# Last delta head: the first half of the output weights folded by GpSimd, and four output products in front of the keys

## The reference

```
qkv = silu(causal_conv4(proj[q, k, v]));  z = proj[z]
q, k = l2norm(q) * 128**-0.5, l2norm(k)
o = chunk_gated_delta_rule(q, k, v, g, beta)            # 8 heads of 128
o = o * rsqrt(mean(o * o) + eps) * onorm_g * silu(z)
out = o.reshape(S, 8 * 128) @ gdn_out_w                 # 1024 x 1024
x = x + gate * out                                      # gate: one row of 1024
```

## Time and profile before

| what | value |
|---|---|
| median of three runs | 2266.24 us (2265.8 to 2268.85) |
| profiled execution | 2268.18 us, span in the trace 2266.1 us |
| TensorE busy | 2176.8 us, 96% |
| VectorE busy | 1311.4 us, 58% |
| ScalarE busy | 593.0 us, 26% |
| GpSimd busy | 172.3 us, 8% |
| head 7 of the delta block | about 1078 to 1220 us of the span |

### The profile page before, as it was taken

How to read it: one execution, slowest core, us unless ns; L and a number is a source line. 1 busy time by engine, 2 the same in 40 slices (tenths; PEclk the granted TensorE clock), 3 DMA queues, 4 the chain that set the end, 5 groups by cost and what they waited for, 6 DMA issues and landing times. The chain is left out here.

```text
span 2266.1 us, 20611 instructions
## 1 busy us (share of the span) xinstructions
PE 2176.8 (96%) x7098; PEld 1120.0 (49%) x7098; DVE 1311.4 (58%) x1833; ACT 593.0 (26%) x960; POOL 172.3 (8%) x135
## 2 busy tenths in 40 slices
PE   6999999989999999999999999999999999999998
PEld 5444444346656656556454455544444444444443
DVE  4687733264664664764823676377469998341333
ACT  4355522233333443443213320121100000230012
POOL 0000000122212212211100000000000000000000
PEclk8999999999999999999999999999999999999999
DMA  9333420121111111111410344321111111015001
GB/s 324 114 110 116 130 103 0 74 65 37 34 26 43 29 33 39 35 32 38 130 32 19 121 64 59 78 76 33 42 33 47 33 33 47 28 37 197 26 19 56
DMA packets 200911, 146.86 MB, mean 65 GB/s; under 512 B 49997, under 2 KB 171906, under 8 KB 200834
## 3 DMA queue, kind: packets, MB, share of 16 engines
q1 hardware_dynamic: 186417, 144.14, 21.6%
q10 hardware_dynamic: 14048, 0.85, 0.4%
q0 software_dynamic: 384, 1.05, 0.2%
HBM read 126.45 MB, written 18.38 MB: 64 GB/s over the span
## 5 line engine op out<-in xcount | busy, mean ns | idle before, releaser
L2095 PE MATMUL bank<-hT,ring 128*128 128x512 f32 x1472 | 637.4, 594 | 2.5 <-DMA ring<-in_w_in 2.5
L2095 PEld LDWEIGHTS bank<-hT,ring 128*128 128x128 f32 x1472 | 279.6, 190 | 352.9 <-issue 349.2
L2756 DVE SCALAR_TENSOR_TENSOR yT<-s_arena,yT 128x1024 f32<-128x1024 f32 x240 | 308.3, 1285 | 8.4
L1235 PE MATMUL bank<-hT,ring 128*128 128x512 f32 x336 | 162.2, 595 | 1.8 <-ACT silu_z L1465 1.8
L2095 PE MATMUL bank<-yT,ring 128*128 128x512 f32 x256 | 110.0, 592 | 0.0
L1810 DVE SCALAR_TENSOR_TENSOR memory<-memory,col_exp_last,bank 128x128 f32<-128x128 f32 x64 | 22.2, 347 | 137.8 <-PE bank L1410 137.8
L2095 PE MATMUL bank<-ssm_y,ring 128*128 128x512 f32 x192 | 83.9, 592 | 0.6 <-DVE s_arena L2770 0.6
L1235 PE MATMUL bank<-resid,yT 128*128 128x512 f32 x168 | 82.5, 593 | 0.0
L2095 PEld LDWEIGHTS bank<-yT,ring 128*128 128x128 f32 x256 | 48.6, 190 | 61.2 <-issue 61.2
L1235 PEld LDWEIGHTS bank<-hT,ring 128*128 128x128 f32 x336 | 56.8, 193 | 36.1 <-issue 36.1
L2399 ACT ACTIVATE s_arena<-bank 128x1024 f32<-128x1024 f32 x8 | 8.2, 1023 | 242.5 <-PE bank L2095 242.5
(11 more groups left out here) (533 smaller groups left out, 3354.4 us busy)
## 6 DMA issues: line engine op xcount, KB each, us to landing
ring<-in_w_in SPq DMA_DIRECT2D x48, 512.0 KB, 3.7
ada<-in_ada_w SPq DMA_DIRECT2D x8, 2048.0 KB, 8.0
ring<-in_gdn_in_w SPq DMA_DIRECT2D x32, 512.0 KB, 4.1
resid<-in_x SPq DMA_DIRECT2D x8, 1024.0 KB, 8.8
ring<-in_lru_in_w SPq DMA_DIRECT2D x16, 512.0 KB, 3.7
lru_arena<-in_ada_w SPq DMA_DIRECT2D x6, 1024.0 KB, 13.1
x_scratch<-resid SPq DMA_DIRECT2D x2, 2048.0 KB, 10.6
decayT<-g_scratch SPq DMA_DIRECT2D x8, 512.0 KB, 4.3
```

The source lines that it names most:

```text
L1235: last = nc.tensor.matmul(bank[:, to, :], w[:, k, :], v[:, k, :], start=(first and k == 0), stop=(k == KB - 1), skip_group_check=not only)
L2095: last = nc.tensor.matmul(bank[:, 2 * PAIR[name] + h, :], w[:, k, :], src[:, k, h * HALF:(h + 1) * HALF], start=(k == 0), stop=(k == kt - 1))
L2756: dve_b.mark(dve.scalar_tensor_tensor(out=yT[:, n, :], in0=padded[:, p, j:j + S], scalar=taps[:, p, j:j + 1], in1=yT[:, n, :], op0=ALU.mul ...
```

## The change

VectorE no longer folds the first half. GpSimd does it, in four operations: tiles 0 and 1 and tiles 2 and 3 after its work for head 6, then the causal addition of head 7, then tiles 4 and 5, then tile 6, then the masks of head 7. Each of the three DMAs of `out_w0` gets a semaphore of its own (`out0_loaded`), each fold raises `folded` by one, and TensorE waits for `folded` at the products k = 0, 2, 4 and 6 of group 0. The first fill of a head, in front of the wait for the keys, takes four products in head 7 instead of none; the other fills keep their counts. GpSimd's `body` is split, so that the masks can be called apart.

```diff
             out_loaded = [sem(f"gdn_out_loaded{n}") for n in range(5)]
+            out0_loaded = [sem(f"gdn_out0_loaded{n}") for n in range(3)]
+            folded = sem("gdn_out0_folded")
...
-                        sp.dma_start(out_w0[:, 2 * b:2 * b + 2, :], out_w[:, 2 * b:2 * b + 2, 0:HALF]).then_inc(out_loaded[0], 16)
+                        sp.dma_start(out_w0[:, 2 * b:2 * b + 2, :], out_w[:, 2 * b:2 * b + 2, 0:HALF]).then_inc(out0_loaded[b], 16)
...
-                    body(HEADS - 1, False, False)
+                    gate = gate_b[:, 1, 0:HALF]
+                    for b in range(2):
+                        g.wait_ge(out0_loaded[b], 16)
+                        g.tensor_tensor(out_w0[:, 2 * b:2 * b + 2, :], out_w0[:, 2 * b:2 * b + 2, :],
+                                        gate.unsqueeze(1).broadcast_to([P, 2, HALF]), ALU.mult).then_inc(folded, 1)
+                    hd_dve.wait(g, "rel", HEADS - 1)
+                    hd_pool.mark(g.tensor_tensor(decayT[:, :, :], decayT[:, :, :], along(causal[:, :]), ALU.add), "rel")
+                    g.wait_ge(out0_loaded[2], 16)
+                    g.tensor_tensor(out_w0[:, 4:6, :], out_w0[:, 4:6, :], gate.unsqueeze(1).broadcast_to([P, 2, HALF]), ALU.mult).then_inc(folded, 1)
+                    g.wait_ge(out_loaded[1], 16)
+                    g.tensor_tensor(out_w6, out_w6, gate, ALU.mult).then_inc(folded, 1)
+                    masks(HEADS - 1)
...
-                            if n == 0:
-                                dve_f.wait(pe, "fold0")
                             if n == TT:
                                 dve_f.wait(pe, "fold1")
                             for k in range(KT - 1):
-                                if (n, k) == (0, 6):
-                                    dve_f.wait(pe, "fold6")
+                                if n == 0 and k % 2 == 0:
+                                    pe.wait_ge(folded, k // 2 + 1)
...
-                        fill(4, 0)
+                        fill(4, 4)
...
-                            fold("fold0", out_w0, gates[0].unsqueeze(1).broadcast_to([P, 6, HALF]), 0, 3)
-                            fold("fold6", out_w6, gates[0], 1, 1)
```

More of the change, by code:

```diff
@@ L1067, in block_program @@
             out_loaded = [sem(f"gdn_out_loaded{n}") for n in range(5)]
+            out0_loaded = [sem(f"gdn_out0_loaded{n}") for n in range(3)]
+            folded = sem("gdn_out0_folded")
             pe_f = Steps(sem("gdn_fill_pe"), [f"part{n}" for n in range(len(GROUPS_OUT))])
-            dve_f = Steps(sem("gdn_fill_dve"), ["fold0", "fold6", "fold1", "fold7"] + [f"sum{n}" for n in range(len(GROUPS_OUT))])
+            dve_f = Steps(sem("gdn_fill_dve"), ["fold1", "fold7"] + [f"sum{n}" for n in range(len(GROUPS_OUT))])
             with nc.Block() as block:
@@ L1177, in weight_sums, with masks @@
                         done.mark(g.tensor_tensor(w["S4"], w["A12"], w["S2"], ALU.subtract), "S4")
-                    def body(h, second, first):
-                        hd_dve.wait(g, "rel", h)
-                        hd_pool.mark(g.tensor_tensor(decayT[:, :, :], decayT[:, :, :], along(causal[:, :]), ALU.add), "rel")
+                    def masks(h):
                         hd_dve.wait(g, "xT", h)
@@ L1188, in body @@
                             hd_pool.mark(g.tensor_tensor(part[n % 2][:, :, :], AT[:, :, :], along(level_mask[:, n, :]), ALU.mult), f"part{s}")
+                    def body(h, second, first):
+                        hd_dve.wait(g, "rel", h)
+                        hd_pool.mark(g.tensor_tensor(decayT[:, :, :], decayT[:, :, :], along(causal[:, :]), ALU.add), "rel")
+                        masks(h)
                         if second:
```

## The result

The changed kernel takes 2273.74 us, the median of 22 runs (2271.33 to 2279.91). The kernel before, run again beside it, takes 2269.84 us, also over 22 runs (2265.8 to 2277.28). The ratio is 1.0019 with a 95% interval of 1.0012 to 1.0025, that is +4.3 us (+2.7 to +5.7): slower by a little, and with its middle just inside the 4.5 us that the prediction took as the bound of "no change". The forecast was +4.0 us.

The account below looks back on a forecast made before the run. TensorE, busy 96% of the span, was taken as the bound. Late fold +1.5, clock after the new wait +1.7, block end -0.2, clock at the next block +1.0 sum to +4.0: 2270.2 us, 8-in-10 range 2266.6 to 2273.3.

Parts of the forecast that it names:

- The absolute time: Whole kernel: +4.0 us on the median of 2266.24 gives 2270.2 us.
- the four products: Last head: they fill 3.43 of 4.14 us idle before the keys; at the head's end they were hidden work.
- the late fold: Fifth output product: waits for GpSimd's fold of tiles 4 and 5 until 1089.1 instead of starting at 1087.63, +1.47 us.
- the clock after the new wait: Products behind the 3.8 us idle after kk: half clock costs +1.7 us, bounds 0 and +2.8.
- the end: Last head's end: earlier loads -0.2 us; half clock on the next block's first tile +1.0, bounds 0 and +1.9.
- Rivals 1 and 4: Clock stays full: only the later fold costs, +1.3 us, chance 0.18; or the pair fold is also cheap, +0.2, chance 0.06.
- Rival 2: Fold, clock and next block's first tile all at their bounds: +7.2 us, 2273.4; chance 0.14.
- Faster: Front of last head: products go on at 1085.3 when kk ends, not 1087.63, -2.3 us, 2263.7; chance 0.04.

Follow-up runs that it names:

- c0_again: hybrid_c0 unchanged, run a second time on the same chip; ratio 0.9964 against the kernel before, -8.2 us.
- late_tail4: Changed kernel with 30 instead of 34 products ahead of the first inverse step, so four stand again at the head's end; ratio 0.9990 to before.
- hybrid: Changed kernel, but GpSimd folds tiles 0 to 3 and 6 before its causal addition, VectorE tiles 4 and 5 after rel; ratio 1.0000 to before.
- front_dummy: Changed kernel plus four products nobody reads right behind kk, in the gap before the fifth product; ratio 1.0013 to before, +3.0 us.
- both_dummy: Changed kernel plus four unread products behind kk and four at the head's end; ratio 0.9997 to before, -0.7 us.
- early_folds: Changed kernel with the folds of tiles 4 and 5 and of tile 6 ahead of GpSimd's causal addition; ratio 1.0017 to before, +3.9 us.
- tail_dummy: Changed kernel plus four products nobody reads at the head's end; ratio 1.0006 to before, +1.4 us.
- no_front: Changed kernel without products in front of the keys, the four back at the head's end, all folds on GpSimd; ratio 0.9997 to before, -0.7 us.
- hybrid_tail4: hybrid with 30 instead of 34 products before the first inverse step and four at the head's end; ratio 0.9986 to before, -3.2 us.
- hybrid_c0: hybrid_tail4 with 28 instead of 30 products before the first inverse step and two in front of the recurrence; ratio 0.9975 to before, -5.7 us.

## Why the prediction was right or wrong

**The absolute time failed, at the base of the sum.** The step was "on the median: 2270.2", with 2266.24 from three runs as base, and a range that took their scatter, 2265.8 to 2268.85, as that of the kernel. Over 22 runs before has a median of 2269.84 and reaches 2277.28. The range went only 3.1 us above the time forecast. With the median of the 22 as base the same sum gives 2273.8, and 2273.74 was measured. What goes with the scatter, the trace of before already showed in part: half-clock stretches behind gaps, which come in some places and not in others. Among the 23 runs of before beside c0_again those with a span of 2275.5 and 2274.8 have a mean clock of 0.985, those with 2264.8 and 2265.4 have 0.990. By estimate from these means, half clock lasts some 68 us in the former and 45 in the latter, and half of the difference, 11 us, is about what they differ by. It is no strict rule (the fastest, 2263.8, has 0.988), and no run changes this scatter on purpose, so that its cause is argued and not shown.

**Right: the four products bring nothing by themselves.** They fill the gap (0.70 us left, predicted 0.7), and `kk` ends at 1085.4 (predicted 1085.3). At the other end the transposes still wait for o_tok. late_tail4 and hybrid show that the same four, taken from a place that was not hidden, are worth 3.4 us.

**Right: the late fold.** Predicted 1089.1, +1.47 us; the fifth product began at 1088.93 on a head that starts 0.06 earlier, +1.36 us. front_dummy and both_dummy show it with the clock kept full: +1.4. The causal addition took 2.35 us, the folds 2.35 and 1.27, with 2.30 us from one start to the next.

**Right in kind, too small for this execution: the clock after the new wait.** The term was +1.7, from half of 3.4 us. In the profiled execution 5.3 us of products ran at half clock, a loss of 2.6 to 2.7 us and close to the upper bound of 2.8, in a stretch that began inside the gap and was longer than most of the earlier ones. So the query transposes came at 1107.14, behind the 1104.5 to 1106.3 that the prediction named. In late_tail4, with the same front, the loss was 1.6, and by the ratios of front_dummy it is 1.4; the term fits these.

**Too small: the end.** The term was +1.0 for the clock and -0.2 for the block's end. Measured in the profiled execution: -0.3 (the next block begins 0.48 us behind y instead of 0.82), +0.9 for the output transposes at half clock, which the sum had left out, and +2.9 for the first tile, where +1.9 was my bound. That bound was wrong: a tile wholly at half clock takes twice its time, 3.7 us more, not half of it more. I had halved the length of work at full clock, where only the length of a slow stretch is to be halved. The other traces with no product at the head's end lost 2.0 to 2.5 us at the tile (early_folds, front_dummy, hybrid), so that +1.0 was too small in all four; tail_dummy gives 3.0 by the ratios.

**Luck in the difference.** The spans of the two profiled executions differ by 6.9 us and not by 4.0. Before's was 1.7 us below its median of 22 and the changed kernel's 1.1 above, which accounts for 2.8 of the 3.0 us between 6.9 and the 3.9 by which the medians moved. That +4.0 met the +4.3 of the runs is therefore in part luck: its terms for the head's end were too small, and what makes the average execution lose less than the profiled one stays open.

**Later in the span** little changes: of the +7.5 at ScalarE's first operation +6.9 are left at the end. TensorE's wait for the weights at 1356, 2.49 us before, is 1.12 us in the changed kernel, and the next one, for `yT` at 1375, grew from 3.10 to 3.78.

**The rivals.** Faster (weights ready when `kk` ends) did not occur; hybrid shows what it would have given: -2.2 in front, where -2.3 was worked out, but 0.0 by its runs, since the rival left out the clock at the end. Rivals 1 and 4 needed full clock behind the new wait, which the trace does not have. Rival 2 (+7.2) lies near the +6.9 of the profiled execution, and the half clock there came close to its prices, but its first condition failed. It had decay_a going between the folds, which did not happen: VectorE's decay_a took 2.17 us, with GpSimd's last fold beside it, and no product waited for tile 6.

## What to carry to other kernels

Work that is moved into a gap is a gain only if it is taken from where the engine does not wait anyway; four products that had covered another wait brought nothing by themselves, and four taken from a busy stretch brought 3.4 us. When a step is handed to another engine, read that engine's queue to the place where the step will stand: here one pair of tiles behind an addition was 3.5 us late. That cost 1.4 us by itself and 1.4 to 2.6 us more by the clock. A time of three runs was a poor base here, 3.6 us off the median of 22: compare ratios.

## What the runs showed of the hardware that was not expected

A gap of 2.23 us before the next block, harmless in the traces of before and late_tail4, is followed by half clock in no_front, hybrid_tail4 and both traces of hybrid_c0, at a cost of 1.6 to 1.7 us each. In tail_dummy half clock lasted some 20 us behind a gap of 4.75 us, with TensorE busy all the time. Half clock lasted 6.8 us in one piece (from 1087.5 to 1094.3) after a gap of 3.5 us, and from 1220.6 to beyond 1230 where two gaps of 3.2 and 1.9 us followed each other. With GpSimd's folds beside VectorE's key taps both became slower in turn: 2.6 us more for the taps, 1.9 us more for the two folds.
